# Who copies the key blocks: ScalarE instead of GpSimd, and the weight-sum transfers in one run

## The reference, cut to what matters

```python
h = modulate(x, g_ffn1, shift0, scale0)
x = x + 0.5 * gate0 * swiglu(h, w_ffn1_up, w_ffn1_down)
h = modulate(x, g_mix, shift1, scale1)
proj = h @ w_in                     # q, k, v of 8 + 8 heads of 64, a gate, a forget logit
o_sb = stick_breaking_attention(sb_q, sb_k, sb_v)
o_fx = forgetting_attention(rmsnorm(fx_q), rmsnorm(fx_k), fx_v, log_f_cum)
x = x + gate1 * (concat(rmsnorm(o_sb), rmsnorm(o_fx) * sigmoid(fox_gate)) @ w_out)
h = modulate(x, g_ffn2, shift2, scale2)
x = x + 0.5 * gate2 * swiglu(h, w_ffn2_up, w_ffn2_down)
return rmsnorm(x, g_final)
```

## Time and profile before

| | |
|---|---|
| Time, median of 3 runs | 1062.82 us (1060.06 to 1065.25) |
| The profiled execution: its own time | 1066.24 us |
| Its span, first to last instruction | 1064.4 us |
| Mean granted clock of TensorE in it | 0.995 of full speed |
| Busy: TensorE, VectorE, ScalarE, GpSimd | 1040.9, 756.4, 561.0, 71.8 us |
| Moved by DMA: queue of SyncE, queue of GpSimd | 163.11 MB, 90.18 MB |

### The profile page before, as it was taken

One profiled execution on the slowest core, in us unless ns is written; L12 is line 12 of the kernel. 1 busy time (PEld: TensorE's weight loads), 2 busy tenths in 40 slices (PEclk: granted clock), 3 DMA queues, 4 the chain that ended last, 5 costly groups with the idle time before them and its releaser, 6 DMA issues.

```text
span 1064.4 us, 17165 instructions
## 1 busy us (share of the span) xinstructions
PE 1040.9 (98%) x6762; PEld 928.4 (87%) x6762; DVE 756.4 (71%) x1083; ACT 561.0 (53%) x901; POOL 71.8 (7%) x108
## 2 busy tenths in 40 slices
PE   8999999999999999999999989999999999999997
PEld 5788888888899999888878767789999999999997
DVE  4656555655888878986886676579866766787973
ACT  6422122122455664876786666458545445466663
POOL 1000000000000002010111111000000000000000
PEclk9999999999999999999999999999999999999999
DMA  9979999999699982685689897799999999789652
GB/s 338 292 235 302 324 316 325 304 281 337 181 315 243 336 252 75 214 277 184 164 176 195 175 184 167 146 266 214 227 307 258 293 258 272 232 211 270 192 163 80
DMA packets 276108, 254.97 MB, mean 240 GB/s; under 512 B 7244, under 2 KB 239804, under 8 KB 273980
## 3 DMA queue, kind: packets, MB, share of 16 engines
q1 hardware_dynamic: 250736, 163.11, 52.9%
q0 software_dynamic: 24832, 90.18, 34.7%
q10 hardware_dynamic: 460, 0.58, 0.2%
HBM read 249.65 MB, written 90.18 MB: 319 GB/s over the span
## 4 chain that ended last, share of the span: by engine, by line
PE 87%; DMA 5%; SPq 3%; ACT 2%; DVE 1%; issue 1%; POOL 0%; ACTq 0%; DVEq 0%
PE bank L1079 27%; PE bank L1081 27%; PE bank L1080 27%; SPq L936 2%; DMA d_raw<-in_w_ffn_down_dram 2%; DMA e_raw<-d_sums 2%; PE bank L1440 1%; PE bank L1412 1%; PE bank L1388 1%; DMA w_raw<-in_w_ffn_up_dram 1%; PE bank L1389 1%; DMA k_hh_a<-k_hh_a 1%; PE bank L1122 1%; DMA k_hh_b<-k_hh_b 0%; PE bank L1390 0%
## 5 line engine op out<-in xcount | busy, mean ns | idle before, releaser
L1079 PE MATMUL bank<-h_hi,w_hi 128*128 128x512 f32 (+1 forms) x592 | 231.4, 391 | 0.0
L1081 PE MATMUL bank<-h_hi,w_lo 128*128 128x512 f32 (+1 forms) x592 | 224.1, 379 | 0.0
L1080 PE MATMUL bank<-h_lo,w_hi 128*128 128x512 f32 (+1 forms) x592 | 224.0, 378 | 0.0
L1608 ACT ACTIVATE w_hi<-w_raw 128x1024 fp32r<-128x1024 f32 x73 | 77.2, 1058 | 190.7 <-PE bank L1081 190.5
L2188 DVE TENSOR_TENSOR w_lo<-w_raw,w_hi 128x1024 fp32r<-128x1024 f32 x73 | 89.3, 1225 | 109.2 <-ACT w_hi L1608 108.6
L1079 PEld LDWEIGHTS bank<-h_hi,w_hi 128*128 128x128 f32 x592 | 112.2, 190 | 24.6 <-issue 2.9
L1080 PEld LDWEIGHTS bank<-h_lo,w_hi 128*128 128x128 f32 x592 | 112.1, 189 | 24.3 <-issue 3.1
L1081 PEld LDWEIGHTS bank<-h_hi,w_lo 128*128 128x128 f32 x592 | 112.0, 189 | 22.8
L2363 DVE TENSOR_TENSOR up_lo<-up_raw,up_hi 128x1024 fp32r<-128x1024 f32 x80 | 86.6, 1086 | 21.7 <-ACT up_hi L1717 21.7
L1081 PE MATMUL bank<-combo,up_lo 128*128 128x256 f32 x320 | 90.7, 283 | 0.0
L1079 PE MATMUL bank<-x_hi,d_hi 128*128 128x256 f32 x308 | 88.2, 286 | 2.5 <-DVE d_lo L2194 2.4
(11 more groups left out here) (320 smaller groups left out, 2550.3 us busy)
## 6 DMA issues: line engine op xcount, KB each, us to landing
d_sums<-in_w_ffn_down_dram POOLq DMA_DIRECT2D x24, 1408.0 KB, 10.0
w_sums<-in_w_ffn_up_dram POOLq DMA_DIRECT2D x24, 1280.0 KB, 8.1
ada_w<-in_w_ada_dram SPq DMA_DIRECT2D x56, 512.0 KB, 8.1
w_raw<-in_w_ffn_up_dram SPq DMA_DIRECT2D x48, 512.0 KB, 10.0
up_raw<-w_sums SPq DMA_DIRECT2D x40, 512.0 KB, 8.4
w_raw<-in_w_in_dram SPq DMA_DIRECT2D x28, 512.0 KB, 4.7
d_sums<-d_sums POOLq DMA_DIRECT2D x8, 1408.0 KB, 14.1
d_raw<-d_sums SPq DMA_DIRECT2D x16, 704.0 KB, 5.3
```

The costliest lines, as they stand in the source:

```text
L1079: mm(dst, wh, xh, start=start, stop=False, skip_group_check=skip)
L1080: mm(dst, wh, xl, start=False, stop=False, skip_group_check=skip)
L1081: return mm(dst, wl, xh, start=False, stop=stop, skip_group_check=skip)
L1608: a(w_hi[:, s, :], w_raw[:, r, :], ACT.Copy).then_inc(w_hi_done, 1)
```

## The change

ScalarE now issues the two transfers of each key block, right behind its own two writes of that block. GpSimd issues no transfers of key blocks any more; all the remaining pieces of `w_sums` follow each other, each waiting only for the one before. One piece of `w_sums` fewer is issued in the first down stage (three instead of four, the first at `T_DOWN1 + 16`). Of the second down stage's pieces, four instead of three come at once behind `w_sums`, the fifth waits for the first four tiles of the second up stage, and each later one has the wait that the piece two places ahead of it had; the last two no longer wait for tiles of the second down stage itself.

```diff
-            def repeat_k(j):
-
-                pool.wait_ge(*k_made(j))
-                g.dma_start(k_hh[j % 2][HD:P, 0, :].bitcast(F32), k_hh[j % 2][0:HD, 0, :].bitcast(F32))\
-                    .then_inc(k_twice[j % 2], 16)
-                g.dma_start(k_hh[j % 2][0:HD, 1, :].bitcast(F32), k_hh[j % 2][HD:P, 1, :].bitcast(F32))\
-                    .then_inc(k_twice[j % 2], 16)
...
-            for n in range(4):
-                copied_after(T_DOWN1 + 13 + 3 * n)
+            for n in range(3):
+                copied_after(T_DOWN1 + 16 + 3 * n)
                 up_pieces(1)
...
                 pool.wait_ge(mix_zero, n + 1)
-                if n == 0:
-                    repeat_k(0)
-            up_pieces(2)
-            for j in range(1, JOBS):
-                repeat_k(j)
-                up_pieces((3, 4, 3, 2, 5, 2, 5)[j - 1])
+            up_pieces(N_PIECES - begun[0])
             for n, piece in enumerate(DOWN_PIECES):
-                if n >= 3:
-                    copied_after(T_DOWN2 + 1 + 4 * (n - 14) if n >= 14 else uses(SEVEN0 + 1 + 3 * (n - 3) // 2, 3))
+                if n == 4:
+                    copied_after(T_UP2 + 2 * SEVEN0)
+                elif n > 4:
+                    copied_after(uses(SEVEN0 + 1 + 3 * (n - 5) // 2, 3))
                 down_piece(1, *piece)
...
+            def repeat_k(j):
+
+                act.wait_ge(*k_made(j))
+                act.dma_start(k_hh[j % 2][HD:P, 0, :].bitcast(F32), k_hh[j % 2][0:HD, 0, :].bitcast(F32))\
+                    .then_inc(k_twice[j % 2], 16)
+                act.dma_start(k_hh[j % 2][0:HD, 1, :].bitcast(F32), k_hh[j % 2][HD:P, 1, :].bitcast(F32))\
+                    .then_inc(k_twice[j % 2], 16)
...
                         last.then_inc(chunk_hi, 1)
                         n_hi += 1
+                        if what == "k":
+                            repeat_k(n)
...
                         last.then_inc(nrm_hi, 1)
+                        if what == "k":
+                            repeat_k(n)
```

## The result

The changed kernel took 1079.78 us (median of 4 runs, 1078.82 to 1081.35) against 1064.03 us (1060.06 to 1065.74) for the kernel before: a ratio of 1.0152, with a 95% interval of 1.0122 to 1.0182. That is on the other side of the forecast of 1057.1, and outside the range. The profiled execution has a span of 1079.5 us against 1064.4.

What follows compares the result with a forecast made beforehand. The kernel was taken as bound by TensorE, busy 1040.9 of 1064.4 us. Terms -4.4 - 2.7 + 0.55 + 0.6 + 0.2 = -5.75 us took the median of 1062.82 to 1057.1 us; range 1053 to 1064.

Steps and rivals of the forecast that it cites:

- Mixer, landing of the copies.: Key-block copies in the mixer, issued by ScalarE, land in 3.4 us, ending TensorE's waits at jobs 6 and 7: 2.7 us won.
- a sign that it would be wrong: In the changed kernel's trace, mixer copies landing 5 us after their issue would show the forecast wrong.
- the 5.10 of job 7: Landing in us of job 7's mixer copy before the change, a piece issued just behind it; upper bound for the landing.
- job 0 and the run of pieces: Mixer start: pieces begin some 5 us earlier, so one is under way with job 0's copy; 0.2 us of wait, 0 to 1.9.
- The margin of 0.3: Mixer, job 0 before the change: copy landed at 424.45, scores began at 424.73, a margin of 0.3 us.
- Nobody waited for them, so this is worth nothing: Mixer: without GpSimd's 40.1 us of waits the pieces are made perhaps 25 us earlier, worth nothing by itself.
- The first rival: Mixer copies land as late as before; nothing won there and 1.35 us paid: 1059.8 us, chance 0.21.
- The second down stage: TensorE's wait for `d_lo` and the slow clock behind it go, as no GpSimd transfer is left there: -4.4 us.
- ScalarE's price: Mixer: ScalarE's waiting and issuing, 0.9 us per job, mostly hidden; 0.55 us at job 4 and 0.6 at six others.
- The rival of 7.2 us: ScalarE's issues delay all eight mixer jobs, 7.2 us of waits plus 1.9 at job 0: 1067.5 us, chance 0.10.
- Slower: Outcome of the rival where ScalarE's issues stand on every mixer job's path: +4.7 us, 1067.5 us, chance 0.10.

Runs made afterwards that it cites:

- without the traffic: Changed kernel with `w_sums` pieces from the mixer on cut to one row of 128 and plain weights loaded in the second up stage: 1060.37 us against 1065.09, ratio 0.9958.
- the new issuer alone: Kernel before, with only the key-block copies moved to ScalarE; GpSimd still waits for each key block at its eight places: 1074.56 us against 1065.09, ratio 1.0083.
- paced by the landing: Kernel before, with ScalarE issuing the copies and GpSimd waiting at its eight places for the copies' landing, not the key block: 1070.62 us against 1062.84, ratio 1.0068.
- the loads held back: Changed kernel with four GpSimd waits put back, and SyncE's two loads waiting for the copies of jobs 6 and 7: 1062.92 us against 1063.37, ratio 0.9986.
- the second down stage's waits alone, repeated: Kernel before, with only the changed waits of the second down stage's 16 pieces, measured again on another chip: 1061.24 us against 1063.37, ratio 0.9978.

## Why the prediction was wrong

**The step that failed: "Mixer, landing of the copies."** It put the landing at 3.4 us, between 2.4 and 5.10, because the copy "leaves that queue" and "has nothing ahead of it". Measured in the changed kernel: 5.4, 8.8, 9.2 and 8.8 us at the four jobs that matter. What is ahead of a copy is not its queue's alone: pieces on GpSimd's queue and loads on SyncE's held it up as well. The prediction had named this as a sign that it would be wrong: copies that land 5 us after their issue. Instead of -2.7 the step gave +10.0 us of waits, and with the clock behind them more: up to 910.00 of the kernel before the loss is 19.3 us, of which the waits for key blocks (10.0), the norm (1.3) and `pt_lo` (1.0) make 12.3. The other 7 us are about what TensorE's clock lost behind the long waits, by an estimate: 0.97 over the 271.85 us of work from 410 to 700, where it was 1.00, is 0.03 x 272 = 8 us.

The rows to see it were there, and read too narrowly. The copy of job 6 took its 6.80 us behind a piece of its own queue, and the piece was blamed, as its queue's. It landed at 621.2; the piece had landed at 618.0, and SyncE's load, issued 0.8 us ahead of the copy, at 621.1. And the 5.10 of job 7, taken as the upper bound ("a piece issued just behind it"), belongs to the load ahead of it, not to the piece behind: the same copy takes 2.6 us once the load is gone and the piece still there. So 5.10 was no bound for a copy beside a piece of 10 us; the bound was the whole landing of a piece.

**The step "job 0 and the run of pieces"** had 0.2 (0 to 1.9) for job 0 and nothing for the rest; job 0 was 2.2. The margin of 0.3 there was also misread: 2.4 is the median of two copies, the second took 2.6 and landed at 424.64, so the margin was 0.1. "Nobody waited for them, so this is worth nothing" weighed only what earlier sums give. What they take is the gaps: GpSimd's 40.1 us of waits kept its pieces away from the copies of jobs 1 and 3, and the wait at job 0 did the same there. With four waits put back, at jobs 0, 3, 6 and 7, the loss was gone. Together with the landings this shows the cause. It is not the number of waits that does it: with all eight, each until the copies' landing, a piece came to lie ahead of job 6, and 0.7% were lost.

**The first rival** had the right object and the wrong size: it let the copies land as late as before, when they could land later by a whole piece. It leaned on the rule of the Trainium skill, "DMA: Bandwidth & Descriptors", Queues, rings and completion order, that the queues take turns packet by packet, and concluded that this "would still let a copy of 128 KB pass a piece of 1280 KB". The same section says that an engine drains a whole packet, typically 9 to 17 descriptors, before it turns to another queue. By that page an adding piece of 1280 KB, 256 rows of 5120 bytes in the trace, leaves each of 16 engines 16 rows, an estimate, and that is about one packet: no turn before its end. In rows of 256 bytes it leaves each 320, by the same estimate many packets. The traces agree with both: the copy lands 0.2 to 0.6 us after the end of an adding piece at jobs 3 to 7 of the changed kernel, and 1.5 to 3.1 us before it with rows of 256 bytes. For rows of 640 bytes no run here shows it.

**Right as forecast.** The second down stage: -4.4 forecast, 4.2 won in the trace, 3.1 and 2.1 us in the medians of two comparisons. ScalarE's price: +1.15 forecast, 1.6 measured without the traffic. The rival of 7.2 us for it was rightly thought small. "Slower" had its chance of 0.10 for that price; slower came, but by another mechanism, so this is no hit.

**What stays open.** Medians and profiled executions part by some microseconds: the kernel with the new issuer alone shows 5.3 us more of waits and has a median 9.5 above, the one paced by the landing 2.2 and 7.8. Their runs spread over 6 to 9 us and the profiled one is among the faster, so what the others waited for isn't seen. A part is TensorE's clock: with the new issuer alone the profiled execution (1068.85 us) has a mean granted clock of 0.998 and the slowest (1078.19) 0.992, which is 0.006 x 1067 = 6 us, an estimate. The order among several transfers ahead wasn't settled: at jobs 6 and 7 of the changed kernel the copy landed 0.2 to 0.6 us after the piece, but 1.1 to 1.3 us ahead of SyncE's load that was issued 0.5 us before it; at job 7 with the new issuer alone it landed 3.1 us before the piece; and at job 4 with the loads held back it landed 1.7 us before a piece issued 1.2 us ahead of it.

## What to carry to other kernels

In this kernel a small transfer that something waits for was about as late as the large transfers under way ahead of it, on any queue: a queue of its own saved the issue and not the landing. Before removing a wait from an engine that "only" issues background transfers, list the urgent transfers that fall into the time in which it stood still, and how much of a background transfer could be ahead of each. Where background transfers can be cut or held for the few urgent moments, hold them (four waits were enough here); making their rows so short (256 bytes) that others can pass cost more than it gave.

## What was not expected of the hardware

- A copy of 128 KB within on-chip memory took 2.4 us alone (issued by ScalarE, the second of two) and up to 9.2 us behind a DRAM-to-DRAM piece of 1280 KB on another queue; in the changed kernel it landed 0.2 to 0.7 us after the piece at seven of eight jobs (job 3: 526.5 and 526.73).
- The same copy waited as well for a load of 512 KB issued 0.5 to 0.8 us ahead (5.1 to 5.7 us), and not at all for a piece issued 0.5 us behind (2.6 us from GpSimd, as alone).
- A copy issued behind a piece was held up only where the piece's rows began ahead of it. An issue on GpSimd took 0.52 us for a plain piece, 1.12 for an adding one in rows of 5120 bytes, 2.0 at 640 bytes and 3.65 at 256. Issued 0.2 us behind a plain piece the copy took 6.9 and 7.4 us, issued 0.2 to 0.3 us behind an adding one 2.4 to 2.5.
- Adding pieces slowed with their rows: 10.2 us at 5120 bytes, 13.6 at 640, 16.7 at 256 (medians of the pieces from `w_sums` to itself).
- Behind a pause of 3.98 us of TensorE its granted clock was 0.66 in the stretch from 525 to 535; over the mixer four such pauses (2.2 to 4.2 us) cost about 8 us beside their own 13.7. Not each pause does so: behind waits of 2.6 and 3.3 us with the new issuer alone the clock over the next 9 us was 1.00, and behind the wait of 2.4 to 2.7 us at job 6 the stretch from 620 to 630 had 1.00 in the kernel before and 0.83 in the profile of the second down stage's waits alone, repeated.
